# Three waits in the third block of a one-core transformer kernel, taken in smaller pieces

## The chip, the core and the metric

The kernel runs on one core of one Trainium2 chip, in float32. The metric is the time of one execution on the device in microseconds (us), median of three runs; lower is better. PE is the matmul engine (TensorE), DVE VectorE, ACT ScalarE, POOL GpSimd, and SP the engine whose queue issues the weight loads.

## What is computed

Three transformer blocks run one after the other on 256 rows of width 1024. The first has a mixer and a mixture of 32 experts, the second retention beside a recurrent layer. The change lies in the third, which has two layers:

```python
def third_block(x, ...):
    # layer 1: gated linear attention, 4 heads of 512 columns
    x = x + gla_mixer(rmsnorm(x))     # ... o = headnorm(o) * silu(z);  return o @ w_out
    # layer 2: S5, a state space model of width 2048
    x = x + s5_mixer(rmsnorm(x))      # as below
    return rmsnorm(x)

def s5_mixer(h, ...):
    u, z = split(h @ w_in)
    lam_bar = exp(lam * dt);  b_coef = (lam_bar - 1) / lam     # coefficients, independent of x
    y = scan over time(u, lam_bar, b_coef * b, c) + d * u
    y = gelu(y)
    y = y * sigmoid(y @ w_glu + b_glu)
    y = y * silu(z)
    return y @ w_out
```

Both `w_out` matrices have 2048 rows (so two chunks of 1024 rows for each half of the 1024 output columns).

## The kernel before

Each engine has its own program, written out by hand, and runs it in its order; engines meet only at semaphores (`ev(name)` is one). The weights come in chunks of 1024 x 512 (2 MB). SP issues them into slots of the tile `W`: six slots before the S5 layer, four of them from its first chunk (number `n5`) on. A load waits until PE has finished the chunk that had the slot before (`chunk_done`). A "unit" is one output of 512 columns in two banks of PSUM (`PS`); units take the two pairs of banks in turn, and `unit_free` says that a pair has been read.

`dense` (L643) computes a unit. In its "row" kind it takes the chunks one after the other, for each the 16 products of 2 row tiles and 8 tiles of the contraction; each product has 512 columns and stands twice in the profile (float32 is done in two passes), so a chunk is 32 records. `dense_by_rows` (L669) finishes the first 128 rows before it begins the second, and calls `between` after the 16 products of the first rows and again in the middle of the second. L666 is the matmul of `dense`, L654 the one of its "col" kind, L681 that of `dense_by_rows`.

The end of the attention layer, on PE: four units `gz0` to `gz3` give the gate z. ACT takes Silu of each (L1611), DVE multiplies it into the heads' outputs `OG` (L2387) and raises `og_ready`. `turn_head(h)` (L1225) transposes head h in eight parts into two banks, and ACT copies them into `OGT` (`copy_head`, L1606), which raises `tp_copied`; `TB["og"] + n` is its count after n copies, two for each head. Then come the output projections `go0` (`dense`) and `go1` (`dense_by_rows`). Contraction tiles 0 to 7 are heads 0 and 1, tiles 8 to 15 heads 2 and 3.

What depends on nothing in this layer but is placed behind it is the setup of S5's coefficients. ACT's program has `copy_head(3)`, and directly after it an Exp (L1616) which raises `s5_setup`. DVE waits for that (ahead of L2392) and runs a chain up to L2484; then it raises `coef_ready` and adds `go0` to `X` (L2301). ACT waits for `coef_ready`, spreads coefficients into `BD` (`spread_b`, L1680, raises `s5_bd`), rounds angles (L1641, L1643), and prepares the first trigonometric tables. PE's `turn_b(ct)` (L1246), the `between` of `go1`, waits for `s5_bd`. POOL waits for all eight copies of `OGT` and then issues four loads of 512 KB (b and c, L618 and L620), which DVE reads from L2462 on.

The S5 layer is a loop of 16 steps. In its step 14, PE begins the gate's first unit `sg0` with the 13 contraction tiles that are ready (`S5_EARLY`), half of the output tiles; ACT has to do Gelu on those 13 tiles of `U16` first (L1753, one instruction of 13 x 256 = 3328 elements). Units `sg1` to `sg3` follow. For each, ACT takes Sigmoid (L1764) and DVE multiplies (L2554) into 4 of the 16 tiles of `G16` and raises `glu_ready`. The last two units, `so0` and `so1`, read `G16`. The places that wait:

```python
            turn_head(3)
            columns_ready("og")
            ...
            dense("go0", lambda k: OGT[:, k, :])
            dense_by_rows("go1", lambda k: OGT[:, k, :], turn_b)
            ...
            pe.wait_ge(ev("glu_ready"), 4)
            dense("so0", lambda k: G16[:, k, :])
```

Of the kernel before, what the change touches and what calls it, by code (L numbers as in the profile page):

```python
# [18 lines left out]
ACT = mybir.ActivationFunctionType  # L19
# [18 lines left out]
GLA_H, GLA_DK, GLA_DV, GLA_C, GLA_R = 4, 128, 512, 64, 16  # L38
GLA_TAU = 16.0
S5_CT, S5_P, S5_I, S5_G, S5_N, S5_EARLY = 16, 64, 16, 64, 128, 13  # L40
PAIRS = 4
MAGIC = 12582912.0
TWO_PI = 6.283185
# [126 lines left out]
def build(nc, A, out):  # L170
# [11 lines left out]
    TB, n = {}, 0  # L182
# [8 lines left out]
    with ExitStack() as ctx:  # L191
# [54 lines left out]
        tp_ready, tp_copied = sem("tp_ready"), sem("tp_copied")  # L246
# [3 lines left out]
        def ev(name):  # L250
            if name not in S:
                S[name] = sem(name)
            return S[name]
# [275 lines left out]
        OGT = BIG[:, 2 * ROW:4 * ROW].rearrange("p (k t) -> p k t", t=T)  # L529
# [108 lines left out]

        @block.tensor
        def _(pe):  # L640
            def dense(name, lhs):

                u, kind, chunks, c0 = UNIT[name]  # L643
                ps = unit_ps(name)
                if u >= 2:
                    pe.wait_ge(unit_free[u % 2], u // 2)
                if kind == "col":

                    for i in range(len(chunks)):
                        pe.wait_ge(w_landed[slot_no(c0 + i)], load_count(c0 + i))  # L650
                    for m in range(4):
                        for i in range(len(chunks)):
                            for k in range(KT):
                                ins = pe.matmul(ps[:, m // 2, (m % 2) * T:(m % 2 + 1) * T],  # L654
                                                slot(c0 + i)[:, k, m * P:(m + 1) * P], lhs(i * KT + k), start=i + k == 0,
                                                stop=i == len(chunks) - 1 and k == KT - 1, skip_group_check=True)
                    ins.then_inc(chunk_done, len(chunks))
                    return
                for i in range(len(chunks)):
                    n = c0 + i  # L660
                    pe.wait_ge(w_landed[slot_no(n)], load_count(n))
                    w = slot(n)
                    last_chunk = i == len(chunks) - 1
                    for t in range(TT):
                        for k in range(KT):
                            ins = pe.matmul(ps[:, t, :], lhs(i * KT + k)[:, t * P:(t + 1) * P], w[:, k, :],  # L666
                                            start=i + k == 0, stop=last_chunk and k == KT - 1)
                    ins.then_inc(chunk_done, 1)
# [136 lines left out]
            def columns_ready(name):  # L805
                pe.wait_ge(tp_copied, TB[name] + dict(TRANSPOSES)[name])
# [412 lines left out]
            def turn_head(h):  # L1219
                pe.wait_ge(ev("og_ready"), h + 1)  # L1220
                for t in range(TT):
                    n = TB["og"] + 2 * h + t
                    pe.wait_ge(tp_copied, n - 1)
                    for j in range(4):
                        ins = pe.transpose(PS[:, 4 + n % 2, j * P:(j + 1) * P],  # L1225
                                           OG[t][:, h * GLA_DV + j * P:h * GLA_DV + (j + 1) * P], ident)
                    ins.then_inc(tp_ready, 1)

            for i in range(4):
# [2 lines left out]
                    pe.wait_ge(ev("og_copied"), 2 * GLA_H)  # L1232
                if i >= 1:
                    turn_head(i - 1)
            turn_head(3)
            columns_ready("og")
            def turn_b(ct):

                pe.wait_ge(ev("s5_bd"), ct + 1)
# [7 lines left out]
                                           BD[ct % 2][:, h, a].rearrange("p q s b i -> p (q s b i)"), ident)  # L1247
                ins.then_inc(ev("s5_turned"), 1)

            dense("go0", lambda k: OGT[:, k, :])  # L1250
            dense_by_rows("go1", lambda k: OGT[:, k, :], turn_b)

            keep_active(6, 4)
# [76 lines left out]
            def gate_part(name, ms, ks):  # L1330

                u, _, chunks, c0 = UNIT[name]
                ps = unit_ps(name)
                for m in ms:
                    for k in ks:
                        ins = pe.matmul(ps[:, m // 2, (m % 2) * T:(m % 2 + 1) * T], slot(c0 + k // KT)[:, k % KT, m * P:(m + 1) * P],  # L1336
                                        U16[:, k, :], start=k == 0 and m % 2 == 0, stop=k == S5_CT - 1, skip_group_check=True)
                return ins
# [8 lines left out]
            for ct in range(S5_CT + 1):  # L1347
                if ct >= 1:
                    from_state(ct - 1)
                if ct + 2 < len(fill):  # L1350
                    fill_half(ct + 2, 0)
                if ct + 2 < S5_CT:
                    turn_b(ct + 2)
                if ct + 2 < len(fill):
                    fill_half(ct + 2, 1)
                if ct + 2 < S5_CT:
                    drive(ct + 2)
                if ct + 1 < S5_CT:
                    within(ct + 1)
                if ct < S5_CT:  # L1360
                    direct(ct)
                if ct == S5_CT - 2:
                    u, _, chunks, c0 = UNIT["sg0"]
                    pe.wait_ge(unit_free[u % 2], u // 2)
                    pe.wait_ge(ev("s5_in"), S5_CT)
                    for i in range(2):
                        pe.wait_ge(w_landed[slot_no(c0 + i)], load_count(c0 + i))
                    pe.wait_ge(ev("s5_gelu"), 1)
                    gate_part("sg0", (0, 1), range(S5_EARLY))
                if ct == S5_CT - 1:  # L1370
                    gate_part("sg0", (2, 3), range(S5_EARLY))
            pe.wait_ge(ev("s5_gelu"), 2)
            gate_part("sg0", range(4), range(S5_EARLY, S5_CT)).then_inc(chunk_done, 2)
            for i in range(1, 4):
                dense(f"sg{i}", lambda k: U16[:, k, :])
            pe.wait_ge(ev("glu_ready"), 4)
            dense("so0", lambda k: G16[:, k, :])
            dense_by_rows("so1", lambda k: G16[:, k, :])


# [1 line left out]
        def _(act):  # L1382
# [354 lines left out]
            for ct in range(S5_CT + 1):  # L1737
                if 2 <= ct + 1 < S5_CT:
                    trig(ct + 1)
                if ct + 1 < len(fill):  # L1740
                    fill_copy(ct + 1)
                if ct < S5_CT:
                    within_copy(ct)
                if ct + 2 < S5_CT:
                    spread_b(ct + 2)
                    rounded(ct + 2)
                    stack_u(ct + 2)
                    turned_copy(ct + 2)
                if ct == S5_CT - 2:
                    act.wait_ge(ev("s5_out"), ct)  # L1750
                    spread_c(ct + 1)
                    act.drain()
                    act.activation(U16[:, 0:S5_EARLY, :], U16[:, 0:S5_EARLY, :], ACT.Gelu_apprx_tanh).then_inc(ev("s5_gelu"), 1)  # L1753
                if ct >= 1:
                    y_out(ct - 1)
                if ct + 1 < S5_CT and ct != S5_CT - 2:
                    spread_c(ct + 1)
# [865 lines left out]
```

## Time and profile before

| | |
|---|---|
| median of three runs | 2227.41 us (2225.69 to 2227.54) |
| the profiled execution | 2228.49 us |
| its span in the trace | 2226.7 us |
| PE busy | 2122.8 us, 95% of the span |
| DVE, ACT, POOL busy | 784.1, 444.5, 76.1 us |
| mean granted PE clock | 0.991 of full speed |

Times inside the trace count from the start of the span. A row of the timeline has the start, the length, the engine, line and operation, what it writes and reads, and how many records are merged; in square brackets stands how long the engine had been idle before it, and what it then waited for. "PEclk 0.50" means that TensorE ran at 1.2 instead of 2.4 GHz.

### The profile page before, as it was taken

The numbers are of one execution on the slowest core, as the hardware profiler recorded it, in microseconds if no ns is written. First come the engines' busy times: TensorE is split into PE (matmuls) and PEld (weight loads), VectorE is DVE, ScalarE is ACT, GpSimd is POOL, SyncE is SP. The second block draws the span as 40 slices with busy tenths as digits, with TensorE's granted clock in tenths as the row PEclk, the third lists the DMA queues.
The fourth block names the chain that finished last, engine by engine and source line by source line (L and its number), as shares of the span: only waits on it lengthen the run. The fifth ranks groups of instructions, "written<-read, shape, count | busy, mean of one in ns | idle before, by whom it ended". The sixth has DMA issues, their size and how long they took to land.

```text
span 2226.7 us, 30826 instructions
## 1 busy us (share of the span) xinstructions
PE 2122.8 (95%) x11636; PEld 1102.8 (50%) x11637; DVE 784.1 (35%) x1910; ACT 444.5 (20%) x895; POOL 76.1 (3%) x96
## 2 busy tenths in 40 slices
PE   6999999999999998999999998999999999998998
PEld 5745553333333333333333336745564446887873
DVE  1894362222222222222222223340212354998100
ACT  1011120111011110101101101132012215997100
POOL 0000000000000000000000000000000000222000
PEclk9999998999999999999999999999999999999999
DMA  9754678989999996999989999435234323232340
GB/s 368 262 189 148 247 288 324 418 342 417 372 402 419 418 418 250 417 390 374 417 354 417 418 418 379 159 114 189 76 128 151 113 95 141 78 115 77 138 156 28
DMA packets 157318, 591.33 MB, mean 266 GB/s; under 512 B 5072, under 2 KB 5136, under 8 KB 124352
## 3 DMA queue, kind: packets, MB, share of 16 engines
q1 hardware_dynamic: 152240, 572.03, 65.7%
q0 software_dynamic: 4384, 16.40, 2.0%
q10 hardware_dynamic: 624, 1.93, 0.2%
q8 instruction: 48, 0.79, 0.1%
q14 instruction: 22, 0.18, 0.0%
HBM read 589.29 MB, written 1.05 MB: 265 GB/s over the span
## 4 chain that ended last, share of the span: by engine, by line
PE 75%; ACT 9%; DMA 6%; DVE 5%; DVEq 1%; issue 1%; SPq 1%; ACTq 1%
PE PS L666 19%; PE PS L1054 15%; PE PS L654 9%; PE PS L1075 9%; DMA W<-in_w_gu 5%; PE PS L697 4%; PE PS L681 4%; PE PS L1087 2%; PE PS L1000 2%; ACT BIG L1691 1%; PE PS L1336 1%; PE PS L1045 1%; PE PS L1017 1%; DVE BIG L2076 1%; DVE BIG L2078 1%
## 5 line engine op out<-in xcount | busy, mean ns | idle before, releaser
L1054 PE MATMUL PS<-W,BIG 128*64 128x512 f32 x2048 | 451.0, 597 | 10.7 <-DMA W<-in_w_gu 10.7
L666 PE MATMUL PS<-W,BIG 128*128 128x512 f32 x960 | 417.9, 597 | 4.3 <-DVE BIG L2554 2.9
L666 PEld LDWEIGHTS PS<-W,BIG 128*128 128x128 f32 x960 | 183.2, 191 | 231.3 <-issue 225.8
L1054 PEld LDWEIGHTS PS<-W,BIG 128*64 128x64 f32 x2048 | 143.8, 137 | 300.6 <-issue 279.6
L1075 PE MATMUL PS<-W,BIG 128*64 128x512 f32 x1024 | 226.8, 595 | 2.8
L654 PE MATMUL PS<-BIG,W 128*128 128x256 f32 x896 | 194.5, 380 | 0.7 <-ACT BIG L389 0.7
L654 PEld LDWEIGHTS PS<-BIG,W 128*128 128x128 f32 x896 | 170.2, 190 | 24.5 <-ACT BIG L389 1.0
L1501 ACT ACTIVATE BIG<-BIG 128x512 f32<-128x512 f32 x32 | 20.2, 630 | 717.3 <-DVE BIG L2076 717.3
L2076 DVE TENSOR_SCALAR BIG<-PS 128x512 f32<-128x512 f32 (+1 forms) x38 | 24.7, 650 | 353.5 <-PE PS L1054 331.5
L1075 PEld LDWEIGHTS PS<-W,BIG 128*64 128x64 f32 x1024 | 70.4, 137 | 138.3 <-issue 125.0
L1273 PE MATMUL PS<-BIG,W 128*128 128x256 f32 x512 | 117.0, 382 | 5.0 <-ACT BIG L1658 3.0
L1273 PEld LDWEIGHTS PS<-BIG,W 128*128 128x128 f32 x512 | 94.9, 190 | 20.4 <-issue 7.7
L1841 DVE SCALAR_TENSOR_TENSOR BIG<-BIG,PC 128x255 f32<-128x255 f32 (+29 forms) x240 | 95.4, 464 | 3.8 <-issue 0.5
L697 PE MATMUL PS<-W,BIG 128*128 128x512 f32 x192 | 83.7, 593 | 0.7 <-ACT BIG L389 0.7
L681 PE MATMUL PS<-W,BIG 128*128 128x512 f32 x192 | 83.2, 592 | 0.0
L2118 DVE TENSOR_TENSOR BIG<-PS,BIG 128x512 f32<-128x512 f32 x32 | 22.1, 692 | 163.3 <-PE PS L1075 163.3
L958 PE MATMUL PS<-BIG 128*64 128x512 f32 x264 | 64.4, 609 | 3.9 <-issue 3.5
L1087 PE MATMUL PS<-BIG 64*128 64x256 f32 x512 | 63.9, 389 | 0.0
L1087 PEld LDWEIGHTS PS<-BIG 64*128 64x128 f32 x512 | 46.9, 186 | 30.2 <-issue 26.0
L681 PEld LDWEIGHTS PS<-W,BIG 128*128 128x128 f32 x192 | 36.4, 190 | 44.9 <-issue 44.9
L697 PEld LDWEIGHTS PS<-W,BIG 128*128 128x128 f32 x192 | 36.1, 190 | 43.5 <-issue 42.5
L2301 DVE TENSOR_TENSOR X<-X,PS 128x512 f32<-128x512 f32 x12 | 8.0, 686 | 126.0 <-PE PS L681 65.3
(508 smaller groups left out, 2012.4 us busy)
## 6 DMA issues: line engine op xcount, KB each, us to landing
W<-in_w_gu SPq DMA_DIRECT2D x128, 2048.0 KB, 15.6
W<-in_w_dn SPq DMA_DIRECT2D x64, 2048.0 KB, 16.1
W<-in_w_in SPq DMA_DIRECT2D x24, 2048.0 KB, 17.7
W<-in_w_mod SPq DMA_DIRECT2D x12, 2048.0 KB, 10.9
W<-in_gla_w_in SPq DMA_DIRECT2D x10, 2048.0 KB, 7.9
W<-in_s_w_in SPq DMA_DIRECT2D x8, 2048.0 KB, 8.8
W<-in_s_w_glu SPq DMA_DIRECT2D x8, 2048.0 KB, 8.5
W<-in_w_out SPq DMA_DIRECT2D x6, 2048.0 KB, 7.9
```

Of the source, the lines that this page charges most:

```text
L654: ins = pe.matmul(ps[:, m // 2, (m % 2) * T:(m % 2 + 1) * T], slot(c0 + i)[:, k, m * P:(m + 1) * P], lhs(i * KT + k), start=i + k == 0, st ...
L666: ins = pe.matmul(ps[:, t, :], lhs(i * KT + k)[:, t * P:(t + 1) * P], w[:, k, :], start=i + k == 0, stop=last_chunk and k == KT - 1)
L681: ins = pe.matmul(ps[:, t, :], lhs(i * KT + k)[:, t * P:(t + 1) * P], w[:, k, :], start=i + k == 0, stop=i == 1 and k == KT - 1)
L697: ins = pe.matmul(unit_ps(name)[:, t, :], lhs(k)[:, t * P:(t + 1) * P], slot(c0)[:, k, :], start=k == 0, stop=k == KT - 1)
L958: ins = pe.matmul(PS[hh[h], 3, :], G[:, t, :], H2[:, t, h * CH:(h + 1) * CH], start=t == 0, stop=t == TT - 1, skip_group_check=True)
L1000: ins = pe.matmul(PS[qq[q], g, 0:T], XETX[:, k, :], gu_w(k)[:, g * D + q * T:g * D + (q + 1) * T], start=False, stop=k == KT - 1, skip_gro ...
L1054: ins = pe.matmul(PS[hh[h], g, :], XET[:, k, :], gu_w(k)[:, g * D + h * CH:g * D + (h + 1) * CH], start=False, stop=k == KT - 1, skip_grou ...
L1075: ins = pe.matmul(PS[hh[h], 2, :], ACTT[:, k, :], dn_w(k)[:, h * CH:(h + 1) * CH], start=k == 0, stop=k == KT - 1, skip_group_check=True)
L1087: ins = pe.matmul(PS[:, 4 + q, t * T:(t + 1) * T], SC[r, t * P:(t + 1) * P], YE[r, (q % 2) * T:(q % 2 + 1) * T], start=False, stop=False, ...
L1273: ins = pe.matmul(PS[:, bank, part * T:(part + 1) * T], slot(c0)[:, k, m * P:(m + 1) * P], lhs(k), start=k == 0, stop=k == KT - 1, skip_gr ...
L1841: ins = dve.scalar_tensor_tensor(cv[:, k, lag:], ya[:, k, 0:T - lag], pcol(r), cv[:, k, lag:], ALU.mult, ALU.add)
L2076: dve.tensor_scalar(GT[:, w], PS[:, 0, w], 7.0, None, ALU.min).then_inc(clipped, 1)
```

## The change

It changes three places. First, `dense` takes a function `ready(i)` that it calls ahead of chunk i. For `go0` the new `heads_turned` makes chunk 0 wait for the copies of heads 0 and 1 alone; the transposes of head 3, and the wait for all copies, now stand between chunk 0 and chunk 1. Second, the Gelu on 13 tiles becomes two instructions, on 5 and on 8 tiles, each with its own increment of `s5_gelu`, and PE's first products of `sg0` are split alike. Third, chunk 0 of `so0` waits for `glu_ready` 2 and chunk 1 for 4.

```diff
+S5_PARTS = range(0, 5), range(5, S5_EARLY)
...
-            def dense(name, lhs):
+            def dense(name, lhs, ready=None):
...
                     w = slot(n)
                     last_chunk = i == len(chunks) - 1
+                    if ready:
+                        ready(i)
...
-            turn_head(3)
-            columns_ready("og")
+
+            def heads_turned(i):
+
+                if i == 0:
+                    pe.wait_ge(tp_copied, TB["og"] + 4)
+                else:
+                    turn_head(3)
+                    columns_ready("og")
+
...
-            dense("go0", lambda k: OGT[:, k, :])
+            dense("go0", lambda k: OGT[:, k, :], heads_turned)
             dense_by_rows("go1", lambda k: OGT[:, k, :], turn_b)
...
-                    pe.wait_ge(ev("s5_gelu"), 1)
-                    gate_part("sg0", (0, 1), range(S5_EARLY))
+                    for part in range(2):
+                        pe.wait_ge(ev("s5_gelu"), part + 1)
+                        gate_part("sg0", (0, 1), S5_PARTS[part])
...
-            pe.wait_ge(ev("s5_gelu"), 2)
+            pe.wait_ge(ev("s5_gelu"), 3)
...
-            pe.wait_ge(ev("glu_ready"), 4)
-            dense("so0", lambda k: G16[:, k, :])
+            dense("so0", lambda k: G16[:, k, :], lambda i: pe.wait_ge(ev("glu_ready"), 2 * i + 2))
...
-                    act.activation(U16[:, 0:S5_EARLY, :], U16[:, 0:S5_EARLY, :], ACT.Gelu_apprx_tanh).then_inc(ev("s5_gelu"), 1)
+                    for part in S5_PARTS:
+                        u = U16[:, part.start:part.stop, :]
+                        act.activation(u, u, ACT.Gelu_apprx_tanh).then_inc(ev("s5_gelu"), 1)
```

On PE, between the last unit of the gate z and `go1`, the program stood like this before (L1225 are the transposes of head 3, L666 the products of `go0`, L681 those of `go1`, L1246 the first `turn_b`; each "x15" or "x3" follows a row with the waits):

```order
L1225 MATMUL PS<-K,BIG 128x128 [waits tp_copied,og_ready]
L1225 MATMUL PS<-K,BIG 128x128 x3
L1225 MATMUL PS<-K,BIG 128x128 [waits tp_copied]
L1225 MATMUL PS<-K,BIG 128x128 x3
L666 MATMUL PS<-W,BIG 128x512 [waits w_landed2,unit_free0,tp_copied]
L666 MATMUL PS<-W,BIG 128x512 x15
L666 MATMUL PS<-W,BIG 128x512 [waits w_landed3]
L666 MATMUL PS<-W,BIG 128x512 x15
L681 MATMUL PS<-W,BIG 128x512 [waits w_landed4,unit_free1]
L681 MATMUL PS<-W,BIG 128x512 x7
L681 MATMUL PS<-W,BIG 128x512 [waits w_landed5]
L681 MATMUL PS<-W,BIG 128x512 x7
```

The same place on PE in the changed kernel, where the same operations are L1228, L669, L684 and L1256:

```order
L669 MATMUL PS<-W,BIG 128x512 [waits tp_copied,w_landed2,unit_free0]
L669 MATMUL PS<-W,BIG 128x512 x15
L1228 MATMUL PS<-K,BIG 128x128 [waits tp_copied,og_ready,w_landed3]
L1228 MATMUL PS<-K,BIG 128x128 x3
L1228 MATMUL PS<-K,BIG 128x128 [waits tp_copied]
L1228 MATMUL PS<-K,BIG 128x128 x3
L669 MATMUL PS<-W,BIG 128x512 [waits tp_copied]
L669 MATMUL PS<-W,BIG 128x512 x15
L684 MATMUL PS<-W,BIG 128x512 [waits w_landed4,unit_free1]
L684 MATMUL PS<-W,BIG 128x512 x7
L684 MATMUL PS<-W,BIG 128x512 [waits w_landed5]
L684 MATMUL PS<-W,BIG 128x512 x7
L1256 MATMUL PS<-K 128x128 [waits s5_bd]
```

The eight transposes of head 3 have moved behind the 16 products of the first chunk of `go0`; the second chunk now has the wait for all copies.

ACT's program is the same there. In the changed kernel it reads, from the Silu of `gz3` on (L1621) over the copies of heads 2 and 3 (L1616, merged to x4) and the Exp of the setup (L1626) to the first `spread_b` (L1690):

```order
L1621 ACTIVATE BIG<-PS 128x2x512 [waits chunk_done]
L1616 ACTIVATE BIG<-PS 128x4x128 [waits tp_ready] x4
L1626 ACT_TABLE_LOAD
L1626 ACTIVATE BIG<-PC 128x64
L1628 ACTIVATE BIG<-BIG 128x64 [waits turns_ready]
L1629 ACT_TABLE_LOAD
L1629 ACTIVATE BIG<-BIG 128x64
L1630 ACTIVATE BIG<-BIG 128x64
L1631 ACT_TABLE_LOAD
L1631 ACTIVATE HSD<-HVE 128x8
L1690 ACTIVATE K<-BIG 64x8x16 [waits coef_ready,kb_ready]
```

Nothing moved on ACT here: the copies of head 3 stand ahead of the setup's Exp as they did before.

## Rows read from the trace of the kernel before

**Rows 1.** The page: its first line.

```profile
span 2226.7 us, 30826 instructions
```

**Rows 2.** Waits of PE: line, waited for: total us, times, longest us.

```profile
PE PS L1336 <- ACT BIG L1753: 3.5, 1, 3.5
```

**Rows 3.** Timeline of PE, end of the attention layer.

```profile
1800.18 1.04 PE L1225 MATMUL PS<-K,BIG 128*128 128x128 f32 x8
1802.79 1.09 PE L1225 MATMUL PS<-K,BIG 128*128 128x128 f32 x8 [1.57 <-DVE BIG L2387]
1804.62 29.43 PE L666 MATMUL PS<-W,BIG 128*128 128x512 f32 x64 [0.74 <-ACT BIG L1606]
1833.88 13.90 PE L681 MATMUL PS<-W,BIG 128*128 128x512 f32 x32
1847.62 0.60 PE L1246 MATMUL PS<-K 128*128 128x128 f32 x4
...
1862.23 1.89 PE L803 MATMUL PS<-K 128*128 128x256 f32 x8
```

**Rows 4.** Timeline of ACT, same stretch.

```profile
1803.48 1.09 ACT L1606 ACTIVATE BIG<-PS 128x512 f32<-128x512 f32 x2 [1.10 <-PE PS L1225]
1804.58 1.28 ACT L1616 ACT_TABLE_LOAD   x1
...
1841.14 1.02 ACT L1680 ACTIVATE K<-BIG 64x128 f32<-64x128 f32 x4 [27.64 <-DVEq L2485]
...
1848.54 1.06 ACT L374 ACTIVATE BIG<-X 128x1024 f32<-128x1024 f32 x1 [3.32 <-DVE X L2301]
...
1863.15 1.06 ACT L374 ACTIVATE BIG<-X 128x1024 f32<-128x1024 f32 x1 [2.40 <-DVE X L2301]
```

**Rows 5.** Timeline of DVE, same stretch.

```profile
1806.16 0.22 DVE L2392 TENSOR_TENSOR BIG<-PC,BIG 128x64 f32<-128x64 f32 x1 [3.44 <-ACT BIG L1616]
...
1819.67 1.23 DVE L2462 TENSOR_TENSOR BIG<-W,BIG 128x1024 f32<-128x1024 f32 x1
...
1839.80 1.22 DVE L2484 TENSOR_TENSOR W<-W,BIG 128x1024 f32<-128x1024 f32 x1
```

**Rows 6.** DMA issues of 1790 to 1870 us: count, KB each, median us from issue to landing.

```profile
W<-in_s_w_in SPq DMA_DIRECT2D x4, 2048.0 KB, 8.9
...
W<-in_s_c_im POOLq DMA_DIRECT2D x1, 512.0 KB, 7.1
```

**Rows 7.** Timeline of POOL and of SP: when those loads are issued.

```profile
1804.86 0.53 POOL L618 DMA_DIRECT2D W<-in_s_b_re  x1 [167.10 <-ACT BIG L1606]
...
1820.34 65.15 SPq L442 DMA_DIRECT2D W<-in_s_w_in  x5
```

**Rows 8.** Windows of 2 us: busy us (count) of PE, PEld, DVE, ACT, POOL, then PEclk, DMA share, GB/s.

```profile
1806.00:1808.00 2.00, 2.00 (x4) 0.84 (x3) 1.60 (x5) 0.13 (x1) 2.00 (x5) 0.50 0.95 328
...
2164.00:2166.00 2.00, 2.00 (x4) 0.85 (x3) 0.00 (x0) 0.00 (x0) 0.00 (x0) 0.50 1.04 396
```

**Rows 9.** Timeline of PE, start of the gate's first unit.

```profile
2039.60 0.33 PE L1302 MATMUL PS<-TAB,MISC 128*32 128x32 f32 x16 [2.04 <-ACT BIG L1700]
...
2044.02 13.11 PE L1336 MATMUL PS<-BIG,W 128*128 128x256 f32 x52 [3.45 <-ACT BIG L1753]
...
2058.62 11.39 PE L1336 MATMUL PS<-BIG,W 128*128 128x256 f32 x52
```

**Rows 10.** Timeline of ACT: the Gelu, and a Silu of another size.

```profile
2040.90 2.98 ACT L1753 ACTIVATE BIG<-BIG 128x3328 f32<-128x3328 f32 x1
...
2072.87 3.62 ACT L1760 ACTIVATE BIG<-BIG 128x4096 f32<-128x4096 f32 x1
```

**Rows 11.** Timeline of DVE: the second product into G16.

```profile
2106.28 1.22 DVE L2554 TENSOR_TENSOR BIG<-BIG 128x1024 f32<-128x1024 f32 x1 [24.03 <-ACT BIG L1764]
```

**Rows 12.** Timeline of PE, the last two units.

```profile
2162.81 29.43 PE L666 MATMUL PS<-W,BIG 128*128 128x512 f32 x64 [2.92 <-DVE BIG L2554]
2192.08 27.63 PE L681 MATMUL PS<-W,BIG 128*128 128x512 f32 x64
```

## The prediction, made before the changed kernel was run

> **What bounds the kernel now.** I read the page first: of a span of 2226.7 us [rows 1] PE is busy 95%, so time can only come from PE's idle stretches. The view of waits sorts these, and in the third block single waits of some 3 us stand out, among them the one for the Gelu [rows 2]. Then I read the timeline of PE around the three edited places. Before `go0` PE is idle 1.57 us for DVE's last product and 0.74 us for ACT's copies [rows 3]; before `sg0` 2.04 and 3.45 us [rows 9]; before `so0` 2.92 us [rows 12]. The reader should see a second thing in the same rows: the block of matmuls behind each gap is too long. `go0` and `so0` take 29.43 us, where the same 64 records of `so1` take 27.63 [rows 3, 12]; the first 52 records of `sg0` take 13.11, the next 52 take 11.39 [rows 9]. The windows say why: behind the gaps the granted clock is 0.50, the 1.2 GHz level, for a while [rows 8]. So a gap costs its length and another 1.8 (29.43 - 27.63), 1.7 or 1.8 us.
>
> Last I read ACT and DVE in the first stretch, because the edit moves work that they wait for.
>
> **Third edit, `so0`.** Chunk 0 reads tiles 0 to 7 of `G16`; the second DVE product that makes them ends at 2106.28 + 1.22 = 2107.5 [rows 11], 52 us ahead. PE can go on where `sg3` ends, at 2162.81 - 2.92 = 2159.89, in the pipelined pace 0.13 us earlier. Chunk 1 comes 13.7 us later, when the fourth product is long there. The gap of 3.05 us goes and with it the slow start of 1.80: **-4.85 us**. No new work, nothing moved past a queue. `so1` and what follows keep their lengths.
>
> **Second edit, Gelu.** 3328 elements take 2.98 us and 4096 take 3.62 [rows 10]: 0.833 ns an element and 0.21 us fixed. Five tiles, 1280 elements, take 1.27 us. Their end comes at 2042.17 instead of 2043.88, so PE starts 1.71 us earlier. The second part (8 tiles, 1.9 us) ends by 2044.1; PE needs at least 4.4 us for its first ten products (11.39 / 26 each), so it doesn't wait again. ACT has 0.1 to 0.2 us more in all, and what stands behind it there is needed only 12 us later. **-1.7 us.** The slow clock stays: PE still sits idle 2.04 and about 1.7 us with little between. I take its loss as unchanged, 1.7 us; the bounds are that it disappears (another -1.7) or doubles (+1.7).
>
> **First edit, `go0`.** What it saves: chunk 0 follows the transposes of head 2 at 1800.18 + 0.87 = 1801.05, in place of 1804.62, and at full clock. It ends at 1801.05 + 13.74 = 1814.79 (13.74 is half of `so1`'s pace, and the step from 1833.88 to 1847.62 [rows 3]). The transposes of head 3, which began at 1802.79, now begin there, **12.0 us later**. PE then waits 0.74 us for their copies as before, has chunk 1 from 1816.6 to 1830.3, and the first half of `go1` until 1844.1. By itself this is a gain of 1847.62 - 1844.1 = 3.5 us at that point.
>
> What it costs lies in ACT's queue. The copies of head 3 ended at 1804.57, and the Exp of S5's setup began with its table load at 1804.58 [rows 4], nothing between. In ACT's program the Exp stands behind these copies, and they now end at 1816.55. DVE was waiting for that Exp already before (3.44 us idle, [rows 5]), and ran without a pause from 1806.16 to 1839.80 + 1.22 = 1841.02. ACT then waited 27.64 us for it and spread the coefficients from 1841.14 to 1842.16 [rows 4], and `turn_b` on PE, at 1847.62, found them 5.5 us old. All of this chain moves by 12.0 us: the coefficients are ready at **1854.15**, while PE stands at `turn_b` at 1844.1. PE waits **10 us**. Cover 5.5, arrival 3.5 earlier, chain 12 later: 12.0 + 3.5 - 5.5 = 10.
>
> From `turn_b` to the end of `go1` it was 1862.23 - 1847.62 = 14.61 us [rows 3]. So the work behind `go1` starts at 1854.19 + 14.61 = 1868.8, which is **+6.6 us**, and after 10 us of idling the second half of `go1` begins at 1.2 GHz as behind every other long gap: **+1.8 us**, between 0 and 3.6 (none, or two of the losses seen). Together **+8.4 us**. The second `turn_b` is not late: ACT's copy of the first is done by about 1859.2, PE comes at 1861.5 or later. ACT's last piece before S5, the norm of the second rows, was reached at 1863.15 - 2.40 = 1860.75; 12.0 later, less the 3.32 us that it formerly waited for the first rows and now doesn't [rows 4], is 1869.4, and PE's chain brings the rows at 1863.15 + 8.4 = 1871.5. ACT stays about 2 us ahead. DVE adds `go0` to `X` 12 us late; nobody waits for it before 1868.
>
> **The loads.** POOL issues its four loads of b and c after the same copies: at 1804.86 before [rows 7], at 1816.8 now. The last landed about 1806.4 + 7.1 = 1813.5 [rows 6], 6.1 us before DVE reads them at 1819.67 [rows 5]. Relative to DVE that stays. But SP's first load of 2 MB for S5, issued at 1820.34 when chunk 0 was done [rows 7], is now issued at about 1814.9, just ahead of them, so the two meet. 4.2 MB where a load of 2 MB takes 8.9 us [rows 6] and the windows show up to 396 GB/s [rows 8] are some 10.6 us of transfer, landed near 1829; DVE reads at 1831.65. Hidden, with under 3 us to spare. The Trainium skill, "DMA: Bandwidth & Descriptors", section "Issuing engines are not separate DMA queues", says the same of any two queues: they run on the same 16 engines and interleave. By that rule the loads slow each other down, and the sum would move only if b and c came more than 2.7 us later than I work out; the rows before never had the two together, so no row shows it.
>
> **Sum.** 8.4 - 1.7 - 4.85 = **+1.8 us**. Against the profiled execution: its 2228.49 us (span 2226.7 and 1.8 us around it) become 2230.3. That execution was 1.1 us above the median of the three runs, so the forecast for the median is 2227.41 + 1.8 = **2229.2 us**. Within 0.2% (4.45 us, about what a measurement of this kernel can tell from no change) that is the same.
>
> On the slow clock: the Trainium skill, "TensorE: Matmul & The Clock Gate", Part 1, "What's actually happening", has two levels, 1.2 GHz after idling and 2.4 GHz after activity, and finds that the count of slow matmuls differs from run to run for the same kernel. By it each of my two remaining losses could come out off the 1.8 us of the rows in any execution; the three rows agree within 0.1 us (1.80, 1.72, 1.80), and I keep 1.8.
>
> **The rivals.**
> *Null result (forecast), 82%.* The setup chain gives back what the other two places win. For it: every link has its row, and ACT's queue has no gap between copy and Exp.
> *Faster, 5%.* The setup isn't on the path: the cover of 5.5 us is larger than the row says, or the chain shortens while PE idles. Then PE loses nothing at `turn_b`, the first edit gains its 3.5 us (the slow start of `go0` is in them), and the time is 2227.41 - 3.5 - 1.7 - 4.85 = 2217.4. Against it: DVE's chain is 34.9 us without a pause, and it cannot begin before the Exp. It decides where the first edit costs under 2.1 us in place of 8.4.
> *Slower, 13%.* The loads of b and c become the end of the chain. Before they took 8.65 us from first issue to last landing; at half speed through the meeting with SP's 2 MB they take 17.3 and land at 1834.1, 2.5 us late: 2231.7. A third more than that, late by 5 us, gives 2234.2. It decides from 2.7 us late on. For it: the slack of 6.1 us shrinks to under 3. Against it: the 2 MB load has a head start of 2 us and is finished after some 6 us of sharing.
> *The edits do nothing* (a chunk still waits as long) would need the copies of heads 0 and 1 or the second product to be late; both are 12 and 50 us early. Then +8.4 would stand alone or less; under 1%, counted with slower.
>
> **Numbers.** The forecast's own range comes from the clock behind the 10 us stall, a loss of 0 to 3.6 us: 2227.4 to 2231.0, and with half a us for the scatter of medians 2226.9 to 2231.5. The range for 8 in 10 takes in some of the bound at `sg0` (-1.7) below, and loads 2.5 us late above: **2226.3 to 2232.3**. Faster 0.05, same 0.82, slower 0.13.
>
> **What would show it.** In the profile of the changed kernel: `so0` without a gap and at 27.6 us; the wait for Gelu about 1.7 us; chunk 0 of `go0` from 1801.1, the Exp's table load at about 1816.6, 12 us later than before; DVE's first product of b and c 12 us later with no wait for a DMA; and before the first `turn_b` an idle PE of 10 us with ACT's spread as its releaser, the clock at 0.50 behind it. No such wait, or one under 5 us, makes this wrong; a DMA named as what DVE waits for makes the slower rival right.

## The result, and the profile after

| | before | after |
|---|---|---|
| median (20 executions each) | 2226.94 us (2223.03 to 2233.11) | 2231.00 us (2227.25 to 2236.43) |
| the profiled execution | 2228.49 us | 2230.53 us |
| its span | 2226.7 us | 2228.6 us |
| PE busy | 2122.8 us | 2121.7 us, 95% |
| DVE, ACT, POOL busy | 784.1, 444.5, 76.1 us | 784.1, 444.6, 76.0 us |

The ratio after to before is 1.0020, with a 95% interval of 1.0013 to 1.0026: 4.5 us more, between 2.9 and 5.8. (Every difference and interval of timed runs below is a ratio times 2227 us; the two medians differ by 4.1 us.) The interval does not hold 1.0000: the change makes the kernel slower, by a fifth of a per cent. The forecast was 2229.2 us, +1.8, in a range of 2226.3 to 2232.3.

The waits of PE in the changed kernel (line, waited for: total us, times, longest us) have a new row, the second of all, and the wait for the Gelu is half as long as it was (1.7 us for 3.5) [rows 2]:

```profile
PE PS L1256 <- ACT K L1690: 9.9, 1, 9.9
...
PE PS L1346 <- ACT BIG L1765: 1.7, 1, 1.7
```

L1256 is the transposition in `turn_b`. The timeline of PE around it, which answers to [rows 3]:

```profile
1799.46 1.04 PE L1228 MATMUL PS<-K,BIG 128*128 128x128 f32 x8
1800.33 13.90 PE L669 MATMUL PS<-W,BIG 128*128 128x512 f32 x32
1814.07 1.04 PE L1228 MATMUL PS<-K,BIG 128*128 128x128 f32 x8
1815.84 14.00 PE L669 MATMUL PS<-W,BIG 128*128 128x512 f32 x32 [0.74 <-ACT BIG L1616]
1829.68 13.90 PE L684 MATMUL PS<-W,BIG 128*128 128x512 f32 x32
1853.44 1.11 PE L1256 MATMUL PS<-K 128*128 128x128 f32 x4 [9.87 <-ACT K L1690]
1854.35 8.40 PE L684 MATMUL PS<-W,BIG 128*128 128x512 f32 x16
...
1869.90 1.89 PE L806 MATMUL PS<-K 128*128 128x256 f32 x8
```

Chunk 0 of `go0` now follows the transposes of head 2 with no gap and at full clock, then come head 3's transposes and chunk 1. Counted from head 2's transposes, PE comes to `turn_b` 3.5 us earlier than it did (43.96 us for 47.44), and loses that and more in front of it: 9.87 us of idling, and behind it 16 records in 8.40 us where 7.03 is the full pace. The window of 2 us there (columns as in [rows 8]) shows the granted clock at 0.50, the 1.2 GHz level:

```profile
1854.00:1856.00 2.00, 2.00 (x5) 1.03 (x4) 0.24 (x1) 1.91 (x7) 0.00 (x0) 0.50 0.00 0
```

Timeline of ACT, the same stretch, against [rows 4]:

```profile
1814.70 1.08 ACT L1616 ACTIVATE BIG<-PS 128x512 f32<-128x512 f32 x2 [13.04 <-PE PS L1228]
1815.81 1.28 ACT L1626 ACT_TABLE_LOAD   x1
...
1852.37 1.02 ACT L1690 ACTIVATE K<-BIG 64x128 f32<-64x128 f32 x4 [27.63 <-DVEq L2497]
...
1870.82 1.06 ACT L375 ACTIVATE BIG<-X 128x1024 f32<-128x1024 f32 x1 [2.31 <-DVE X L2313]
```

and of DVE, against [rows 5]:

```profile
1817.39 0.22 DVE L2404 TENSOR_TENSOR BIG<-PC,BIG 128x64 f32<-128x64 f32 x1 [15.38 <-ACT BIG L1626]
...
1818.61 2.32 DVE L2411 TENSOR_SCALAR BIG<-BIG 128x64 f32<-128x64 f32 x1
...
1830.90 1.23 DVE L2474 TENSOR_TENSOR BIG<-W,BIG 128x1024 f32<-128x1024 f32 x1
...
1851.03 1.22 DVE L2496 TENSOR_TENSOR W<-W,BIG 128x1024 f32<-128x1024 f32 x1
```

ACT does nothing for 13.04 us, because the copy of head 3 stands first in its queue; the Exp is directly behind that copy, as before. DVE idles 15.38 us in place of 3.44 for it, and then needs just as long as before (from 1817.39 to 1852.25 it is 34.86 us, before 34.86). The idle time of 27.63 us before the spread is what it was: the whole chain is only shifted.

The last load of b and c, against [rows 6] (columns as there), its issue on POOL, and SP's first load for S5, against [rows 7]:

```profile
W<-in_s_c_im POOLq DMA_DIRECT2D x1, 512.0 KB, 10.7
...
1817.64 0.53 POOL L621 DMA_DIRECT2D W<-in_s_c_im  x1
...
1814.26 48.89 SPq L443 DMA_DIRECT2D W<-in_s_w_in  x3
```

The load was issued at 1817.64, 3.4 us behind SP's, and took 10.7 us instead of 7.1; it landed at 1828.3, and DVE read them at 1830.90, 2.6 us later and with no wait.

The other two places, timeline of PE, against [rows 9, 12]:

```profile
2049.99 13.97 PE L1346 MATMUL PS<-BIG,W 128*128 128x256 f32 x52 [1.75 <-ACT BIG L1765]
...
2166.56 27.63 PE L669 MATMUL PS<-W,BIG 128*128 128x512 f32 x64
```

`so0` has no gap and takes 27.63 us. The wait for the Gelu is 1.75 us, but the 52 records behind it took 13.97 us here, where it was 13.11.

The account of after less before, by the starts of the same work in the two traces: -0.72 us at head 2's transposes, ahead of every edit; +7.67 behind `go1` (1869.90 less 1862.23), so **+8.39** for the first edit; +6.83 at the block behind the Gelu's (2065.45 less 2058.62), -0.84 in all from there for the second edit; +1.95 at `so1` (2194.03 less 2192.08), **-4.88** for the third. The spans differ by 1.9 us, and the stretches from head 2's transposes to the end of the span by 2.6.

### The profile page after: what moved, and what is told of

Read it like the earlier page. It is cut to its first block, busy times and chain, and to the rows that moved or that the text cites. A ratio compares the mean times of both kernels' runs of the same rounds, so it can differ in the third digit from the quotient of the medians.

```text
span 2228.6 us, 30828 instructions
## 1 busy us (share of the span) xinstructions
PE 2121.7 (95%) x11636; PEld 1102.6 (49%) x11637; DVE 784.1 (35%) x1910; ACT 444.6 (20%) x896; POOL 76.0 (3%) x96
## 4 chain that ended last, share of the span: by engine, by line
PE 74%; ACT 9%; DMA 6%; DVE 6%; DVEq 2%; issue 2%; SPq 1%; ACTq 1%
PE PS L669 18%; PE PS L1057 15%; PE PS L655 9%; PE PS L1078 9%; DMA W<-in_w_gu 5%; PE PS L700 4%; PE PS L684 3%; PE PS L1090 2%; PE PS L1003 2%; ACT BIG L1701 1%; PE PS L1346 1%; PE PS L1048 1%; PE PS L1020 1%; DVE BIG L2088 1%; DVE BIG L2090 1%
## 5 line engine op out<-in xcount | busy, mean ns | idle before, releaser
L669 PE MATMUL PS<-W,BIG 128*128 128x512 f32 x960 | 414.6, 592 | 1.4 <-ACT BIG L1616 0.7
L669 PEld LDWEIGHTS PS<-W,BIG 128*128 128x128 f32 x960 | 181.8, 190 | 225.6 <-issue 223.4
L684 PE MATMUL PS<-W,BIG 128*128 128x512 f32 x192 | 84.6, 600 | 0.0
L684 PEld LDWEIGHTS PS<-W,BIG 128*128 128x128 f32 x192 | 37.0, 194 | 45.8 <-issue 45.8
L1003 PE MATMUL PS<-W,BIG 128*32 128x256 f32 x768 | 44.2, 390 | 6.6 <-DVE BIG L2098 6.6
## 6 DMA issues: line engine op xcount, KB each, us to landing
W<-in_w_in SPq DMA_DIRECT2D x24, 2048.0 KB, 17.7
```

The costliest lines, as they stand in the source:

```text
L1003: ins = pe.matmul(PS[qq[q], g, 0:T], XETX[:, k, :], gu_w(k)[:, g * D + q * T:g * D + (q + 1) * T], start=False, stop=k == KT - 1, skip_gro ...
```

## The experiments

Twelve runs in three groups of four (e1 to e4, e5 to e8, e9 to e12), each group on a chip of its own; the runs of a group share their executions of the kernel before, whose medians were 2226.84, 2225.91 and 2227.04 us. The main theory: the first edit holds back S5's setup through ACT's queue and costs some 8 us, which the other two edits give back. The rivals: PE's loss has another cause (the coupling to ACT's queue is not it, or the loads are), or the gain at `so0` is not there.

### One edit at a time

**e1_so0_only.** The kernel before with the third edit alone:

```diff
+                    if ready:
+                        ready(i)
...
-            pe.wait_ge(ev("glu_ready"), 4)
-            dense("so0", lambda k: G16[:, k, :])
+            dense("so0", lambda k: G16[:, k, :], lambda i: pe.wait_ge(ev("glu_ready"), 2 * i + 2))
```

> The kernel before with the third edit alone: chunk 0 of so0 waits for two products, chunk 1 for four. The theory that the three edits are independent (theory A) expects 4.9 us less than before: the idle 2.9 us ahead of so0 gone, so0 at 27.6 in place of 29.4 us. If the measured +4 us of the full change holds something beyond its first edit (theory B, a cost that none of my terms has), this edit or the next could show it: less than 3 us gained here.

Measured 2222.06 us, ratio 0.9979 (0.9970 to 0.9988): -4.7 us (-6.7 to -2.7). Timeline of PE:

```profile
1804.77 27.73 PE L668 MATMUL PS<-W,BIG 128*128 128x512 f32 x64 [0.74 <-ACT BIG L1607]
...
2158.09 27.63 PE L668 MATMUL PS<-W,BIG 128*128 128x512 f32 x64
```

The second row is `so0`, as forecast. The first is `go0`, which this kernel doesn't change: behind the same two gaps it took 27.73 us where the trace of before has 29.43. The slow start that I had taken for a fixed price was missing. The window in which the trace of before has a granted clock of 0.50 [rows 8] has 1.00 here:

```profile
1806.00:1808.00 2.00, 2.00 (x6) 0.88 (x5) 1.45 (x5) 0.28 (x2) 2.00 (x5) 1.00 0.90 295
```

**e2_gelu_only.** The kernel before with the second edit alone:

```diff
-                    pe.wait_ge(ev("s5_gelu"), 1)
-                    gate_part("sg0", (0, 1), range(S5_EARLY))
+                    for part in range(2):
+                        pe.wait_ge(ev("s5_gelu"), part + 1)
+                        gate_part("sg0", (0, 1), S5_PARTS[part])
...
+                    for part in S5_PARTS:
+                        u = U16[:, part.start:part.stop, :]
+                        act.activation(u, u, ACT.Gelu_apprx_tanh).then_inc(ev("s5_gelu"), 1)
```

> The kernel before with the second edit alone, the Gelu in two instructions. Theory A expects 1.7 us less than before in the gap, with a loss to the 1.2 GHz level behind it that may be 1 us smaller or larger: -0.7 to -2.7 us, near what these runs can tell. Theory B, in which the slow clock behind the shorter gap lasts longer and takes the gain back, expects no difference or up to 1 us more, and a block of 52 records behind the gap of 14 us in place of 13.1.

Measured 2226.49 us, 0.9998 (0.9989 to 1.0007): -0.4 us (-2.4 to +1.6), which tells -1.7 neither from 0 nor from -2. The trace is closer: from the start of the 16 small matmuls ahead of the Gelu's wait to the end of the 52 records of `sg0` (the start of what follows them) it is 16.26 us, where the trace of before has 17.46 (2039.60 to 2057.06). So the gain from the second edit is seen in traces alone, not in timed runs.

**e3_go0_only.** The kernel before with the first edit alone:

```diff
-            turn_head(3)
-            columns_ready("og")
+            def heads_turned(i):
+                if i == 0:
+                    pe.wait_ge(tp_copied, TB["og"] + 4)
+                else:
+                    turn_head(3)
+                    columns_ready("og")
...
-            dense("go0", lambda k: OGT[:, k, :])
+            dense("go0", lambda k: OGT[:, k, :], heads_turned)
```

> The kernel before with the first edit alone, the transposes of head 3 between the chunks of go0. Theory A expects 8.4 us more than before (6 to 11), all of it at the first turn_b: PE idle 10 us, released by ACT's spread of coefficients, which is 12 us late. Theory B (the change carries a further 2 us somewhere) would give over 10 us here if the further cost belongs to this edit. If the loads of b and c set the end, DVE's L2462 would wait for a DMA.

Measured 2237.95 us, 1.0048 (1.0034 to 1.0062): +10.7 us (7.6 to 13.8). The loss is that of the first edit alone. It lies above 10 us, where theory B put it, but its interval (5 executions) holds the 8.4 as well, so these runs don't decide between the two. The trace has the same wait of 9.85 us, and 8.91 us for the 16 records behind it.

**e4_before_again.** The kernel before, unchanged.

> The kernel before once more, unchanged, as a control. Both theories expect a ratio of 1.000; how far it falls from that, and how the second trace differs from the first (in the blocks behind the three gaps above all), says what of the 2 us between my sum and the measured medians is scatter. My guess: within 1 us, with blocks behind the gaps that differ by up to 1.7 us between the traces.

Measured 2227.67 us, 1.0004 (0.9995 to 1.0013): +0.9 us (-1.1 to +2.9). So differences of one us can't be told in such a run. In its trace `go0` and `so0` took 29.43 us and the Gelu's block 13.11, as in that of before.

**e8_so0_gelu.** The changed kernel without its first edit:

```diff
-            def heads_turned(i):
...
+            turn_head(3)
+            columns_ready("og")
...
-            dense("go0", lambda k: OGT[:, k, :], heads_turned)
+            dense("go0", lambda k: OGT[:, k, :])
```

> The second and third edit without the first. Theory A expects the sum of the two, -1.0 -4.9 = -5.9 us against before (-5 to -7), and so 10 us less than the full change. If the edits disturb each other, less than -4.9.

Measured 2219.38 us, 0.9973 (0.9962 to 0.9984): -6.0 us (-8.5 to -3.6), within the error the sum of the two edits apart (-5.1). With the first edit added that is the changed kernel at +4.5 (+3.6 in e9): the first edit costs about 10 us by this pair too.

### The coupling through ACT's and POOL's queues

**e5_go0_act_early.** The first edit alone, with the setup's Exp and the four activations that follow it ahead of the copy of head 3 in ACT's program. Its results go into space that head 3's data doesn't use, but the products of b and c do, so DVE waits for that copy ahead of them; POOL's loads stay behind all eight copies:

```diff
-            copy_head(3)
-
             act.activation(work[0], PC[:, 4, 0:64], ACT.Exp).then_inc(ev("s5_setup"), 1)
...
             act.activation(HSD[:, 0:8], HVE[:, 0:8], ACT.Sqrt)
+            copy_head(3)
...
             dve.wait_ge(ev("s5_bc_landed"), 64)
+            dve.wait_ge(tp_copied, TB["og"] + 8)
```

> The first edit alone, with the five ACT instructions of the coefficient setup moved ahead of the copies of head 3, and DVE waiting for the last of these copies only where it begins to overwrite what the transposes read (ahead of L2462 of before). POOL still issues its loads of b and c after the last copy. Theory A (ACT's queue held the setup back, and the loads are the next to be late) expects DVE's small operations to start 12 us earlier than in the first edit alone, but L2462 to wait for the loads, which land about 1828.3: the chain is then 2.6 us shorter and PE's stall at the first turn_b 7.3 us in place of 9.9. Time: 2.6 us under the first edit alone, so 6 to 8 us above before. A theory in which the queue is not the cause (theory B: PE or DVE slower in itself there) expects the same as the first edit alone, +8 to +11 us.

Measured 2233.58 us, 1.0035 (1.0023 to 1.0047): +7.8 us (5.1 to 10.5). Timeline of DVE:

```profile
1803.63 0.23 DVE L2400 TENSOR_TENSOR BIG<-PC,BIG 128x64 f32<-128x64 f32 x1 [1.25 <-ACT BIG L1623]
...
1828.83 1.23 DVE L2471 TENSOR_TENSOR BIG<-W,BIG 128x1024 f32<-128x1024 f32 x1 [14.13 <-DMA W<-in_s_c_im]
```

and of PE:

```profile
1851.37 1.11 PE L1255 MATMUL PS<-K 128*128 128x128 f32 x4 [7.43 <-ACT K L1688]
1852.28 8.44 PE L683 MATMUL PS<-W,BIG 128*128 128x512 f32 x16
```

The setup begins early (1803.63), but DVE then waits for the loads, which are now what is late. The stall shrinks only from 9.85 to 7.43 us. This is the rival "the loads become the end of the chain" with its place and price: in the changed kernel it stood 2.6 us behind the one that decided.

**e6_go0_act_pool_early.** As e5, and POOL issues its loads after six copies in place of eight:

```diff
                 if name == "s5_norm_3":
-                    pool.wait_ge(tp_copied, TB["og"] + 8)
+                    pool.wait_ge(tp_copied, TB["og"] + 6)
```

> As the run before, and POOL waits for six of the eight copies in place of all, so that b and c are loaded 14 us earlier. Theory A expects L2462 at about 1816.8, right behind the last copy, the coefficients spread at 1839, no wait at turn_b at all, and from the transposes of head 2 to the end of go1 58.6 us in place of 61.6 (mean of the four traces without the first edit) or 70.7 (with it): 3 us faster than before, -1 to -5. Theory B expects +5 us or more.

Measured 2224.11 us, 0.9994 (0.9985 to 1.0002): -1.3 us (-3.3 to +0.4). Timeline of PE:

```profile
1799.47 1.04 PE L1227 MATMUL PS<-K,BIG 128*128 128x128 f32 x8
...
1843.42 0.60 PE L1255 MATMUL PS<-K 128*128 128x128 f32 x4
1843.86 7.03 PE L683 MATMUL PS<-W,BIG 128*128 128x512 f32 x16
...
1858.04 1.89 PE L805 MATMUL PS<-K 128*128 128x256 f32 x8
```

No wait at `turn_b`, and 58.57 us from head 2's transposes to the work behind `go1`, where the trace of before has 62.05 (1800.18 to 1862.23) and that of after 70.44. The two queues account for the whole loss, and the first edit freed from them gains its 3.5 us against that trace of before (2.8 against the mean of the five traces without the edit, below). The timed gain of 1.3 us is less than the 3 us expected, and its interval just holds no change.

**e7_all_act_pool_early.** The changed kernel with the two moves of e6.

> All three edits of the change with the setup on ACT ahead of the copies of head 3 and POOL's loads after six copies. If the terms add: -3.0 (go0) -1.0 (Gelu, by the traces) -4.9 (so0) = 8.9 us less than before, some 2218 us. If the slow clock behind the gaps swings, 7 to 10.5.

Measured 2219.73 us, 0.9970 (0.9959 to 0.9982): -6.7 us (-9.1 to -4.0), just short of the 7 to 10.5 us that were expected. **e11_all_early_again** is the same kernel in the third group:

> All three edits with the early setup and loads, a second time, as the partner of the run before on the same chip. Its first comparison gave -0.3% (-6.7 us) where the sum of the terms is -8.9: expected -7 to -10.

Measured 2218.86 us, 0.9964 (0.9950 to 0.9977): -8.0 us (-11.1 to -5.1).

**e9_after_again.** The changed kernel, once more.

> The changed kernel once more, unchanged. Its first comparison gave +0.2% (+4 us), where my sum from the corrected terms (go0 +9.2, Gelu -1.0, so0 -4.8) gives +3.4 and the forecast was +1.8. If the rest is scatter, this gives +2 to +5 us, and the stretch from the transposes of head 2 to the end of the span is 429 us within 1.5. A systematic further cost would show as +4 us or more again with a stretch over 430.

Measured 2231.51 us, 1.0016 (1.0007 to 1.0024): +3.6 us (1.6 to 5.3). The stall was 9.87 us, with 8.46 behind it; the Gelu's block 13.98.

### The clock's part

**e12_after_awake_stall.** The changed kernel, in which PE runs 21 of the kernel's own matmuls that keep it awake (42 records; nobody reads their results) inside the stall; nothing is left out:

```diff
             def turn_b(ct):

+                if ct == 0:
+                    keep_active(6, 21)
                 pe.wait_ge(ev("s5_bd"), ct + 1)
```

> The changed kernel with 21 matmuls on constants (9.2 us, results unread) in the 10 us in which PE waits at the first turn_b. It takes the slow clock away from the stall and leaves the stall: the half of go1 behind it takes 7.0 us in place of 8.4 or 8.9, so the kernel is 1.4 to 2.4 us faster than the changed one, +1 to +3 us against before. If it were as slow as the changed kernel, the block behind the stall would be slow for another reason than the idling.

Measured 2228.16 us, 1.0004 (0.9996 to 1.0013): +0.9 us (-0.9 to +2.9), against 2231.51 for the changed kernel in the same group. Timeline of PE:

```profile
1842.63 9.23 PE L806 MATMUL PS<-K 128*128 128x256 f32 x42
1852.67 0.66 PE L1258 MATMUL PS<-K 128*128 128x128 f32 x4 [0.81 <-ACT K L1692]
1853.16 7.03 PE L684 MATMUL PS<-W,BIG 128*128 128x512 f32 x16
```

The wait ends where it did (53.99 us behind the start of head 2's transposes, 53.98 in the trace of after), but the block behind it is back at 7.03 us and the transposition at 0.66 instead of 1.11. From head 2's transposes to the work behind `go1` it is 68.65 us (70.44 and 70.50 without). So 1.8 of the 9 us are the clock, as the forecast had it, and the rest is the wait. The ratios of the timed runs put 2.7 us between e12 and e9, with intervals that overlap; in the trace of e12 the stretch around the Gelu is shorter by another 0.8 us (15.80 for 16.62 and 16.63), and whether that has to do with the edit is not shown.

**e10_all_early_awake.** As e7, with seven such matmuls (14 records) in the two gaps in front of `sg0`, four in the first and three in the second:

```diff
+                if ct == S5_CT - 2:
+                    wait_fill_read(pe, len(fill) - 1)
+                    keep_active(5, 4)
...
+                    keep_active(5, 3)
```

> All three edits with the early setup and loads, and seven matmuls on constants (results unread) in the two gaps ahead of the gate's first unit: four where PE waits 2.04 us for ACT, three in the 1.75 us ahead of the Gelu. If the long block behind these gaps is the clock's doing, and the gaps are too short to lose it once they are filled, the 52 records take 11.4 us in place of 13.1 to 14.4, and the kernel is 1.7 to 2.6 us faster than the same without them: 9 to 12 us under before. If the block is slow for another reason (its operands just written by ACT, say), it stays at 13 us or more and nothing is gained.

Measured 2216.62 us, 0.9951 (0.9938 to 0.9964): -10.9 us (-13.8 to -8.0), the fastest of all. Timeline of PE in this kernel:

```profile
2035.95 1.99 PE L806 MATMUL PS<-K 128*128 128x256 f32 x8
...
2038.72 1.46 PE L806 MATMUL PS<-K 128*128 128x256 f32 x6
2040.63 11.46 PE L1346 MATMUL PS<-BIG,W 128*128 128x256 f32 x52 [0.45 <-ACT BIG L1769]
```

and in e11, without them:

```profile
2038.80 13.09 PE L1346 MATMUL PS<-BIG,W 128*128 128x256 f32 x52 [1.75 <-ACT BIG L1764]
```

The 52 records take 11.46 us, the pace of the block behind them (11.39). So the extra length of `sg0`'s first block is the clock's doing. The windows of 2 us behind the gap say it directly (columns as in [rows 8]), first e10:

```profile
2040.00:2042.00 2.00, 1.55 (x8) 1.25 (x7) 1.85 (x4) 2.00 (x2) 0.00 (x0) 1.00 0.08 29
```

then e11:

```profile
2040.00:2042.00 2.00, 2.00 (x6) 1.53 (x6) 1.91 (x4) 1.48 (x6) 0.39 (x1) 0.50 0.00 0
```

The granted clock is 1.00 (2.4 GHz) with the gap filled and 0.50 (1.2 GHz) without. In the second case PE is busy for all of the 2 us and has 6 records in them; in the first it is busy for 1.55 us and has 8. That e10 is faster than e11 is plain in the trace (1.6 us in this block); the timed runs, 2216.62 and 2218.86 us, agree, but their intervals overlap.

## Why the prediction was right, and what was off

**The mechanism held, and the time lies in the range.** The median of 2231.00 us is inside 2226.3 to 2232.3. But "the same" meant within 4.45 us of no change, and the measured +4.5 (2.9 to 5.8) stands on that edge and is clear of zero: the kernel is slower, by as much as the forecast was ready to call nothing. Each step that the prediction had named shows in the changed kernel:

| | forecast | measured |
|---|---|---|
| chunk 0 behind the transposes | no gap, full clock, 1801.05 | 1800.33 (0.72 earlier, as all there), 13.90 us, no gap |
| setup's table load later by | 12 us | 1815.81 less 1804.58, and 0.72 for the earlier start: 11.95 |
| PE's wait at `turn_b` | 10 us | 9.87 |
| behind `go1` | +8.4 us | +8.39 |
| slow start behind the stall | 1.8 us (0 to 3.6) | 8.40 - 7.03 = 1.4, and 0.5 in the transposition |
| b and c landed before they are read | 2.7 us | 2.6 |
| ACT's lead at the second norm | about 2 us | 2.31 |
| wait for the Gelu | about 1.7 us | 1.75 |
| `so0` | -4.85 us | -4.88 |

The causes are shown and not only argued: e3 has the loss alone, e6 takes it away by the order in the two queues (its added wait on DVE costs nothing: there is no idle time ahead of the products), e12 separates the clock's 1.8 us from it, and e1 has the gain at `so0` alone. Only the Gelu's term rests on traces without a timed run that is clear of zero.

**The size was off by 2.7 us**, with +4.5 (2.9 to 5.8), and +3.6 (1.6 to 5.3) in e9, for +1.8. The trace of after agrees with the forecast to 0.1 us in two terms of three, so the part of the fault that can be found lies in taking one execution for all, above all in the sentence "the three rows agree within 0.1 us (1.80, 1.72, 1.80), and I keep 1.8". The traces of the experiments, put together, give the terms anew:

- *The first edit, +8.4.* From head 2's transposes to the work behind `go1` it was 62.05, 60.35, 61.82, 62.05 and 60.36 us in the five traces without the edit (before, e1, e2, e4, e8), mean 61.3. Two of these have no slow start in `go0`. With the edit it was 70.44, 70.93 and 70.50 (after, e3, e9), mean 70.6. The term is **+9.3**: the slow start that the edit removes wasn't always there to remove. The timed runs say +10.7 (7.6 to 13.8).
- *The Gelu, -1.7.* From the 16 small matmuls to the end of the 52 of `sg0` it was 17.46, 17.37, 17.73, 17.47, 17.48 and 18.75 us with one Gelu (before, e1, e3 to e6), mean 17.7, and 16.62, 16.26, 15.72, 15.80, 16.63, 15.75 and 15.80 with two (after, e2, e7, e8, e9, e11, e12), mean 16.1. That is **-1.6**, as forecast, but in the profiled execution of after only -0.84.
- *`so0`, -4.85.* Behind the gap of 2.92 us the unit took 29.43 us in five traces (before and e2 to e5) and 27.73 in one (e6); without it, 27.63 in all eight. On the mean **-4.6**.

These sum to 9.3 - 1.6 - 4.6 = +3.1 us, inside both measured intervals. It is an estimate from means over a few traces, some of other kernels; the two traces each of the two kernels themselves say less: from head 2's transposes to the end of the span it was 426.5 and 426.7 us before (before, e4), 429.1 and 429.3 after (after, e9), so +2.6. The 1.4 us left from 3.1 to 4.5 can't be given to a term: e4, the kernel before against itself, came out at +0.9. So of the miss of 2.7 us, 0.9 is the first edit's term, 0.4 the two others', and 1.4 stays open.

**The rivals.** "Faster" (the setup is not on the path) fell at once; it is what e6 and e7 make of the kernel by moving the setup off it. "Slower, by the loads" did not happen, by 2.6 us, and e5 shows its price when the first chain is shortened and the loads are not. The time alone could not have ruled it out: 2231.00 us is nearer to its 2231.7 than to the forecast's 2229.2. What rules it out is DVE's row at 1830.90, which has no wait. One step of that rival's price is wrong as recorded: a third more than 17.3 us is 23.1, which would be 8.2 us late and not 5; the forecast doesn't use it. The meeting of the loads cost what the prediction worked out (landed 1828.3, forecast near 1829). That meeting with SP's load slows them is what five traces show: where the two meet, the last took 10.6 to 10.8 us (after, e3, e5, e9, e12), in place of 7.1 in the trace of before and 6.5 in e6, which has the early loads.

## What to carry to other kernels

Before moving a producer (here the transposes of head 3) behind other work, read what stands behind its consumers in their own queues: ACT's and POOL's work for the next layer had nothing to do with head 3 and still waited for it, and that turned a gain of some 3 us into a loss of 9. When such a coupling is cut, cut it in all the queues at once, and look for the next one that is late: the order in ACT alone was worth 2.6 us of 12 (e5), with POOL's it was all of them (e6). And price the slow clock behind a short gap as something that is sometimes there, from several executions; one profile of each kernel was good to about 2 us here.

## What the runs showed of the hardware

**A short gap costs the slow clock most times, not always.** The same code behind the same gaps gave two lengths for `go0` and `so0`, with little between: `go0` behind 1.57 and 0.74 us took 29.43, 27.73, 29.21, 29.43 and 27.73 us; `so0` behind 2.92 us took 29.43 five times and 27.73 once; the 52 records of `sg0` took 13.0 to 14.4, and 11.46 with the gaps filled. The Trainium skill, "TensorE: Matmul & The Clock Gate", Part 1, "What's actually happening", had said that the count of slow matmuls differs from run to run, and these rows agree.

**A small DVE instruction took 2.32 us in place of 0.20 beside POOL's memsets.** Timeline of DVE in e5, where POOL's memsets come 14 us later:

```profile
1804.61 0.20 DVE L2407 TENSOR_SCALAR BIG<-BIG 128x64 f32<-128x64 f32 x1
```

and of POOL in the changed kernel, where the same instruction is the one of 2.32 us at 1818.61 shown above:

```profile
1818.68 0.54 POOL L624 MEMSET K<- 128x512 f32 x1
...
1820.54 0.33 POOL L627 MEMSET OW<- 128x256 f32 x1
```

The instruction of DVE ends at 1820.93, with the last memset (1820.87). It was 2.31 to 2.33 us in all thirteen traces in which the two meet, and 0.20 in e5. The Trainium skill, "SBUF — State Buffer", section "SBUF: two separate sides", says that a DVE instruction in one of its two-port modes and a GpSimd instruction exclude each other from a shared pair of ports, each for a whole instruction. The rows agree in that the two did not run side by side; that the DVE instruction, whose record begins 0.07 us ahead of the first memset (times on POOL are rough), lasted over all five memsets and not one, the page doesn't say, and which mode it runs in no row shows. By the rows about 2.1 us of the 9.87 us stall would be these memsets, which stand right behind POOL's loads. That is an estimate: in e5 the loads' issues moved away together with the memsets, and a kernel with the memsets alone elsewhere was not run.

**Executions of one kernel differ before they reach the change.** Head 2's transposes start at 1799.46 us in the trace of after and at 1805.52 in that of e9, the same kernel; over all traces it was 1796.75 to 1805.52. From there to the end of the span the two took 429.1 and 429.3 us. Differences of this size between single profiles say nothing of an edit, but the stretch behind a common point does.
